# Attention of a hybrid encoder: heads begun under the input projections, windowed heads turned by a product with a diagonal

## The reference, cut to what matters

```
h = rms_norm(x) * (1 + scale) + shift
qa,ka,va,qd,kd,vd = split(h @ w_in)            # rotary on q and k
windowed (8 heads, 2 kv heads, width 64):  p = exp(s - m) / (sum + exp(sink - m));  o = p @ v
differential (4 heads of 2 maps, width 128): a = softmax(s1) - lam * softmax(s2);  o = rms_norm(a @ v)
x = x + gate * (concat(windowed, differential) @ w_out)
```

## Time and profile before

| | us |
|---|---|
| median of three runs | 1367.25 (1365.81 to 1367.95) |
| profiled execution | 1363.22 |
| its span | 1361.5 |
| TensorE busy | 1288.9 (95%) |
| VectorE, ScalarE busy | 452.0, 292.9 |
| mean granted TensorE clock | 0.984 |

### The profile page before, as it was taken

The page is one execution under the profiler, slowest core; times in us unless marked ns, Lnnn a source line. Parts: engine busy times, 40 slices in busy tenths (PEclk is TensorE's granted clock), DMA queues, the critical chain, the costliest instruction groups (busy, mean ns, idle before and its releaser), DMA issues.

```text
span 1361.5 us, 21859 instructions
## 1 busy us (share of the span) xinstructions
PE 1288.9 (95%) x9514; PEld 714.5 (52%) x9515; DVE 452.0 (33%) x808; ACT 292.9 (22%) x524; POOL 32.8 (2%) x82
## 2 busy tenths in 40 slices
PE   5999999999999989996689999999999999899997
PEld 5766888787888677441233333444354333244342
DVE  4876867777459665200100120001001110000011
ACT  3346544443433462110010000010010000010010
POOL 1102100000001010000000000000000000000000
PEclk9999999999999999998789999999999999899999
DMA  9988748888436757999999999999999999999996
GB/s 349 326 338 329 233 176 311 311 297 309 174 123 208 307 204 306 378 408 424 418 421 423 422 421 419 403 408 421 423 419 421 421 424 421 419 420 421 422 423 259
DMA packets 93044, 481.95 MB, mean 354 GB/s; under 512 B 8808, under 2 KB 10928, under 8 KB 63248
## 3 DMA queue, kind: packets, MB, share of 16 engines
q1 hardware_dynamic: 88992, 475.06, 86.9%
q10 hardware_dynamic: 2720, 2.93, 0.8%
q0 software_dynamic: 1232, 2.50, 0.8%
HBM read 477.32 MB, written 1.05 MB: 351 GB/s over the span
## 4 chain that ended last, share of the span: by engine, by line
PE 82%; DMA 9%; DVE 4%; SPq 2%; ACT 2%; issue 1%; POOL 0%; DVEq 0%; ACTq 0%
PE ps L2621 31%; PE ps L2671 15%; PE ps L2304 8%; PE ps L2306 8%; PE ps L2305 8%; DMA raws<-in_moe_w_down_dram 5%; DMA raw<-in_moe_w_gate_dram 2%; DMA weights<-in_ada_w_dram 2%; SPq L891 2%; PE ps L2687 2%; PE ps L2638 1%; DVE weights_lo L1376 1%; PE ps L2594 1%; PE ps L2385 1%; PE ps L2226 1%; PE ps L2370 1%
## 5 line engine op out<-in xcount | busy, mean ns | idle before, releaser
L2621 PE MATMUL ps<-raw,hX 128*32 128x384 f32 (+3 forms) x3840 | 473.0, 543 | 11.8 <-DMA raw<-in_moe_w_up_dram 8.4
L2621 PEld LDWEIGHTS ps<-raw,hX 128*32 128x32 f32 (+1 forms) x3840 | 162.0, 117 | 296.6 <-issue 267.3
L2671 PE MATMUL ps<-raws,m_actT 128*32 128x512 f32 (+1 forms) x1072 | 168.5, 604 | 9.9 <-DMA raws<-in_moe_w_down_dram 9.9
L2304 PE MATMUL ps<-weights_hi,hT_hi 128*128 128x512 f32 (+1 forms) x416 | 162.1, 390 | 2.6 <-DVE hT_lo L1482 1.4
L1797 DVE TENSOR_TENSOR m_act<-m_act,ps 128x512 f32<-128x512 f32 (+1 forms) x28 | 17.4, 621 | 432.0 <-PE ps L2621 431.2
L2306 PE MATMUL ps<-weights_hi,hT_lo 128*128 128x512 f32 (+1 forms) x416 | 159.0, 382 | 0.0
L2305 PE MATMUL ps<-weights_lo,hT_hi 128*128 128x512 f32 (+1 forms) x416 | 158.6, 381 | 0.0
L1376 DVE TENSOR_TENSOR weights_lo<-weights,weights_hi 128x2048 fp32r<-128x2048 f32 (+1 forms) x52 | 113.1, 2202 | 2.3 <-ACT weights_hi L1052 1.1
L2671 PEld LDWEIGHTS ps<-raws,m_actT 128*32 128x32 f32 (+1 forms) x1072 | 52.2, 123 | 116.3 <-issue 103.5
L1052 ACT ACTIVATE weights_hi<-weights 128x2048 fp32r<-128x2048 f32 (+1 forms) x48 | 87.2, 1840 | 55.9 <-PE ps L2306 51.3
L2304 PEld LDWEIGHTS ps<-weights_hi,hT_hi 128*128 128x128 f32 x416 | 78.2, 188 | 21.0 <-issue 4.8
(11 more groups left out here) (282 smaller groups left out, 1084.3 us busy)
## 6 DMA issues: line engine op xcount, KB each, us to landing
raw<-in_moe_w_gate_dram SPq DMA_DIRECT2D x64, 1024.0 KB, 16.5
raw<-in_moe_w_up_dram SPq DMA_DIRECT2D x64, 1024.0 KB, 22.1
raws<-in_moe_w_down_dram SPq DMA_DIRECT2D x32, 2048.0 KB, 24.7
raw<-in_moe_w_gate_dram SPq DMA_DIRECT2D x64, 768.0 KB, 23.3
raw<-in_moe_w_up_dram SPq DMA_DIRECT2D x64, 768.0 KB, 21.1
raws<-in_moe_w_down_dram SPq DMA_DIRECT2D x28, 1536.0 KB, 19.5
weights<-in_ada_w_dram SPq DMA_DIRECT2D x19, 2048.0 KB, 10.0
weights<-in_ffn_w_gate_dram SPq DMA_DIRECT2D x14, 1024.0 KB, 5.1
```

The lines of the kernel that those rows point to most:

```text
L2304: pe.matmul(dst, stat_hi, hi, start=start, stop=False, skip_group_check=True)
L2621: mm = pe.matmul(ps[tile * q:tile * q + tile, bank, 0:COL[n]], hX[:, i, at_row:at_row + tile], raw[buffer][:, at:at + COL[n]], start=(i == ...
L2671: mm = pe.matmul(ps[tile * q:tile * q + tile, bank, col:col + w], stationary[:, at_row:at_row + tile], rows_in[:, D * j + w * g:D * j + w ...
```

## The change

- **Head of the attention under the projections** (`HEAD_EARLY`, both layers): the turns of q and k, in a new order (`TURN_PAIRS`), the scores of steps 0 and 1 and the first modulation chunk are woven into the input products (3,1), (4,0) and (4,1). ScalarE makes all copies of q and k.
- **Windowed heads**: VectorE multiplies the identity by the reciprocals (`diag`), and TensorE's turn is a product of the probabilities with it, so they come out turned and scaled. `values` holds v stationary (64 columns) and streams the probabilities of both token halves, two heads side by side in the two column halves; the outputs come out turned and are split straight into `hTh` and `hTl` (`window_high`, `head_out`). Two of four turns of outputs fall away, and so do the `keep` products.
- **Output product (0,0)** runs in pieces between steps 6 and 7 (`first_out`). The weights of the second output chunk are split inside the attention in layer 1 (`OUT_SECOND_EARLY`), behind the last turn in layer 0.
- Modulation chunks move to later steps. The mask is added only where it can bite. Squares of the norm move to VectorE, and GpSimd's gate DMAs stand between its two powers.

```diff
-ADA_STEP = [[0, 1, 2, 3, 4, 5, 6, 7], [0, 1, 2, 3]]
+HEAD_EARLY = (True, True)
+ADA_STEP = [[1, 2, 3, 4, 5, 6, 7, 8], [1, 3, 5, 6] if HEAD_EARLY[1] else [0, 1, 2, 3]]
+OUT_SECOND_EARLY = (False, True)
...
+TURN_PAIRS = [(3, 5, 4, 0, 2, 6, 1) if early else tuple(range(QK_TILES // 2)) for early in HEAD_EARLY]
+ROPES_OF_PAIR = (4, 4, 4, 4, 6, 6, 8)
+PAIRS_OF_STEP = ((3, 5), (4, 6), (0, 2), (1, 2))
+BEFORE_HEAD = [IN_ORDER.index((3, 1)) if early else len(IN_ORDER) for early in HEAD_EARLY]
...
-                spread_gate(layer, 0)
                 for t in range(NT):
+                    if t:
+                        spread_gate(layer, 0)
...
+            def attention_head(layer):
+
+                for i in range(4):
+                    copy_qk(layer, i)
+                if layer == 0:
+                    lambda_exp()
+                straight_part("out", layer, 0, 0)
+                exponentials(layer, 0)
+                copy_qk(layer, 4)
+                copy_qk(layer, 5)
+                straight_part("out", layer, 0, 1)
+                copy_qk(layer, 6)
+                exponentials(layer, 1)
...
+                for j in range(2 if early else 0, PAIRS + 3):
+                    k = j - 2
                     if j == PAIRS:
-                        turned_high(3 * layer + 1, 0)
                         turned_high(3 * layer + 1, 1)
+                    if 0 <= k < PAIRS:
+                        copy_probs(k, 0)
+                    if k >= 1 and windowed(k - 1):
+                        window_high(k - 1)
+                    if 0 <= k < PAIRS and windowed(k):
+                        copy_probs(k, 1)
                     if j < PAIRS:
-                        u, q, par = PAIRS * layer + j, j % 4, j % 2
-                        act.wait_ge(max_done, u + 1)
-                        for n in range(4):
-                            e = act.activation(E[:, par, n, :], score_rows(par)[:, n, :], ACT.Exp,
-                                               bias=negm[:, q, n:n + 1], scale=SCALE, accum_out=sums[:, q, n:n + 1])
-                        if pair(2 * j) < 4:
-                            e = act.activation(sinke[:, q, :], sinkm[:, q, :], ACT.Exp)
-                        e.then_inc(exp_done, 1)
+                        exponentials(layer, j)
+                    if j == PAIRS and OUT_SECOND_EARLY[layer]:
+                        straight_part("out", layer, 1, 0)
+                turned_high(3 * layer + 1, 3)
+                if not OUT_SECOND_EARLY[layer]:
+                    straight_part("out", layer, 1, 0)
+                straight_part("out", layer, 1, 1)
...
-                    then(dve.tensor_tensor(rows, rows, mask[:, t, :].unsqueeze(1).broadcast_to([P, 4, SEQ]), ALU.add))
+                    far = slice(P - t * P, 2 * P - t * P)
+                    then(dve.tensor_tensor(rows[:, :, far], rows[:, :, far],
+                                           mask[:, t, far].unsqueeze(1).broadcast_to([P, 4, P]), ALU.add))
...
-                    dve.reciprocal(rec[:, q, :], den[:, q, :]).then_inc(probs_done, 1)
+                    then(dve.reciprocal(rec[:, q, :], den[:, q, :]))
+                    dve.tensor_tensor(diag[:, par], ident[:].unsqueeze(1).broadcast_to([P, 4, P]),
+                                      rec[:, q, :].unsqueeze(2).broadcast_to([P, 4, P]),
+                                      ALU.mult).then_inc(probs_done, 1)
...
+                        square, diff = xn[:, t, 0:WIN_WIDTH], xn[:, t, WIN_WIDTH:]
+                        then(dve.tensor_tensor(square, diff, diff, ALU.mult))
+                        then(dve.reduce_sum(ssq_d[:, four], square.rearrange("p (h n) -> p h n", h=N_DIFF), AX_X))
...
+                    if j == PAIRS + 1 and OUT_SECOND_EARLY[layer]:
+                        low_of("out", layer, 1, 0)
+                    if j == PAIRS + 2:
+                        turned_low(3 * layer + 1, 3)
+                        if not OUT_SECOND_EARLY[layer]:
+                            low_of("out", layer, 1, 0)
...
+                early = HEAD_EARLY[layer]
+                if early:
+                    maxima(layer, 0)
+                    low_of("out", layer, 0, 0)
                 rope(layer, 3, 1)
-                low_of("out", layer, 0, 0)
+                if early:
+                    probabilities(layer, 0)
+                else:
+                    low_of("out", layer, 0, 0)
                 rope(layer, 4, 0)
+                if early:
+                    maxima(layer, 1)
                 rope(layer, 4, 1)
+                if early:
+                    low_of("out", layer, 0, 1)
...
+                        if windowed(j):
+                            row = 2 * (n // 2) + half
+                            mm = pe.matmul(ps[:, 3, n * P:n * P + P], E[:, j % 2, row, keys], diag[:, j % 2, row, :],
+                                           start=True, stop=True)
+                        else:
+                            mm = pe.transpose(ps[:, 3, n * P:n * P + P], E[:, j % 2, n // 2, keys], ident[:])
...
+                    if windowed(j):
+                        col = (m // 2) * HEAD
                         for kt in range(NT):
-                            mm = pe.matmul(ps[:, j % 2, to:to + width], PT[:, i % 2, 2 * h + kt, :],
-                                           v[:, kt, col:col + width], start=(kt == 0), stop=(kt == NT - 1))
+                            for h in range(2):
+                                mm = pe.matmul(ps[HEAD * h:HEAD * h + HEAD, j % 2, 0:2 * P], v[:, kt, col:col + HEAD],
+                                               turned[:, :, 2 * h + kt, :], start=(kt == 0), stop=(kt == NT - 1),
+                                               skip_group_check=True)
...
+                if early:
+                    turn_qk(0)
+                    project("in", layer, 3, 1, range(0, 2))
+                    turn_qk(1)
+                    project("in", layer, 3, 1, range(2, 4))
+                    turn_qk(2)
+                    turn_qk(3)
+                    scores_of(0)
+                    project("in", layer, 3, 1, range(4, KD))
+                    project("in", layer, 4, 0, range(0, 4))
+                    turn_qk(4)
+                    project("in", layer, 4, 0, range(4, KD))
+                    turn_qk(5)
+                    project("in", layer, 4, 1, range(0, 4))
+                    scores_of(1)
+                    turn_qk(6)
+                    project("in", layer, 4, 1, range(4, KD))
+                    pe.wait_ge(qkT_done, 7 * layer + 7)
+                    ada_chunk(*ADA_LATER[layer][0])
+                    pe.wait_ge(rope_done, 2 * IN_CHUNKS * (layer + 1))
...
+                for j in range(2 if early else 0, PAIRS + 3):
                     if j < PAIRS:
                         scores_of(j)
+                    k = j - 2
+                    if 0 <= k < PAIRS:
+                        turn_probs(k, 0)
+                    if j == PAIRS:
+                        first_out(range(0, 2))
+                    if k >= 1:
+                        values(k - 1)
                     if j == PAIRS + 1:
-                        pe.wait_ge(mod_ready, 3 * layer + 3)
-                        keep(5, 2)
-                    a = 2 * (j - 2)
-                    if 0 <= a < UNITS:
-                        turn_probs(a)
-                    if a >= 2:
-                        values(a - 1)
-                    if 0 <= a < UNITS:
-                        turn_probs(a + 1)
-                        values(a)
+                        first_out(range(4, 6))
+                    if 0 <= k < PAIRS and windowed(k):
+                        turn_probs(k, 1)
+                    if j == PAIRS:
+                        first_out(range(2, 4))
+                    if j == PAIRS + 1:
+                        first_out(range(6, KD))
                     for c, (of, n) in enumerate(ADA_LATER[layer]):
                         if ADA_STEP[layer][c] == j:
                             ada_chunk(of, n)
                     if j == PAIRS - 1:
                         pe.wait_ge(mix_done, N_DIFF * (NT * layer + 1))
                         pe.wait_ge(exp_done, PAIRS * layer + PAIRS - 1)
-                        turn_rows_of(3 * layer + 1, 0)
                         turn_rows_of(3 * layer + 1, 1)
+                pe.wait_ge(mix_done, N_DIFF * (NT * layer + 2))
+                turn_rows_of(3 * layer + 1, 3)
```

226 lines of the change are left out of this document (126 added, 100 removed).

## The result

The changed kernel takes 1370.47 us (median of 10 runs, 1365.41 to 1372.01) against 1366.13 us for the kernel before on the same chip (1363.82 to 1369.88): ratio 1.003, 95% interval 1.0019 to 1.0041. The forecast was 3.2 us faster, 1364.0; it is some 4 us slower, outside the range.

The account below looks back on a forecast made before the run. The expert phase was taken as bound by its weight stream, its start tied to TensorE in the mixers. Layer 1's 4.9 plus layer 0's 0.3 less 2.0 for the clock gave 3.2 us, so 1364.0; own range 1362 to 1366.

Parts of the forecast that it names:

- 0.7 us of waiting in the walk, up to 3: Layer 0's attention: six later modulation chunks land about when used, so TensorE waits 0.7 us, up to 3.
- The walk: Step-by-step run through three engine queues in both mixers, each instruction starting when ready; trusted to a microsecond for known operations.
- layer 0's chunks land late: Rival: layer 0's last three modulation chunks each land 1 us later than forecast, giving 1367 us; chance 0.1.
- waits on DMA for modulation weights in layer 0: Sign named in advance that would show the forecast wrong, in layer 0's attention; no size given.
- the sum: Layer 0, (3,1) to (1,0): TensorE work 62.9 us plus waits 1.2 and 5.0, starting at 71.45 and ending at 140.6.
- the late split: Before layer 0's output product (1,0): TensorE idles 5.0 us because its weights are split only behind the last turn.
- the clock behind it: Behind layer 0's 5 us wait the granted clock falls, costing 2.0 us, between none and 2.4.
- the windowed turns and values: Windowed steps, both layers: eight turns as diagonal products take 1.9 us a step, values with v stationary 1.06.
- layer 1's waits: Layer 1's mixer: TensorE waits 2.1 us at step 3, 1.6 at step 8 and 2.2 for (1,0)'s second half.
- The column halves overlap: Rival claimed they do not: windowed values take 1.85 us instead of 1.06, giving 1370.1 us, slower; chance 0.1.
- The rival by which the stream does not start earlier: Expert weight stream's head, not TensorE, sets the rate, so the end moves by 0.3 us: 1367; chance 0.1.
- Layer 1: Layer 1's mixer, (3,1) to (1,0): forecast 4.9 us gained, (1,0) at 505.2 to 505.5 against 510.4.

Follow-up runs that it names:

- chunks_quarter: Changed kernel loading only a quarter of each of layer 0's modulation chunks 6 to 11, same TensorE work; total 1717.93 us says nothing, as tokens go to other experts.
- loads_in_gap: Changed kernel with ScalarE's transfers of router weights, final scale and biases issued earlier, in layer 0's head; 1367.73 us, 1.0009 of the kernel before.
- fillers: Changed kernel with 36 ident by ident products in layer 0's 4.90 us wait and 16 in layer 1's 2.07 us wait; 1370.90 us.
- head0_off: Changed kernel with layer 0's head as in the kernel before, layer 1 keeping the whole change; 1365.72 us, 0.9992 of the kernel before.
- chunks_in_head: Changed kernel with modulation chunks 4 and 5 used inside layer 0's head and their slots refilled at once; 1367.98 us, 1.0013 of the kernel before.
- split0_early: Changed kernel with layer 0's second output chunk split before the last turned rows, as in layer 1; 1364.04 us, 0.9988 of the kernel before.
- heads_off_split: Changed kernel with both layers' heads as before, layer 0's split early and 9 fillers in its wait; 1362.62 us, 0.9975 of the kernel before.
- four_repairs: Changed kernel with chunks 4 and 5 in layer 0's head, chunk steps reordered, layer 0's early split with 9 fillers, and layer 1's VectorE swap; 1357.85 us.
- the swap: Changed kernel with VectorE doing step 1's probabilities ahead of step 2's maxima in layer 1; alone 1366.62 us, 1.0005 of the kernel before.
- four_without_fill: Same as four_repairs but without the 9 fillers in the middle of layer 0's (1,0); 1357.83 us, 0.9944 of the kernel before.

## Why the prediction was wrong

**The step that failed** is the one that put layer 0's chunks at "0.7 us of waiting in the walk, up to 3". They waited 6.17 us, and chunks_quarter puts their price at 6.5. The walk had the cause, spare slots that come free with the last input product, and the pace: from the first (101.14) to the last (131.54) the six chunks land 6.1 us apart. It had three other terms wrong. The slots were to come free 17.4 us after the start of (3,1) (88.8 less 71.45); it was 18.3 (91.14 less 72.86). The first chunk was to follow at the pace of the others, 6.1 us; it took 10.0, with a second chunk, the router weights, the final scale and the biases in flight beside it (without these three 7.7, and (1,0) 2.2 us earlier, in loads_in_gap). And the steps were to take about 6 us; the two ahead of the waits at 120.55 and 126.61 take 4.6 and 4.5 without them. The rival "layer 0's chunks land late" was the right mechanism, sized at 3 us and given 0.1, and "waits on DMA for modulation weights in layer 0" stood among the signs of being wrong.

**Layer 0's head** has a second error, 0.99 us before the sixth turn of q and k. Its chain can be read on ScalarE (first two rows) and VectorE:

```profile
78.36 1.28 ACT L1145 ACT_TABLE_LOAD   x1
79.65 0.21 ACT L1145 ACTIVATE lame<-lams 128x4 f32<-128x4 f32 x1
```

```profile
79.89 0.16 DVE L1482 TENSOR_TENSOR neglam<-lame 128x2 f32<-128x2 f32 x1 [2.39 <-ACT lame L1145]
...
85.48 0.42 DVE L1636 COPY v<-ps 128x256 f32<-128x256 f32 x1
```

The exponential of lambda now stands behind ScalarE's four copies, and a table load comes right ahead of it. Before, that load lay in ScalarE's idle time:

```profile
67.34 1.28 ACT L1310 ACT_TABLE_LOAD   x1
```

VectorE waits 2.39 us for the exponential, where it waited 0.27 before, and then goes without a recorded wait through the maxima, the split and the rotation up to the copy of v that TensorE waits for. No run moves the exponential alone, so this cause is read from the trace and not tested. With the other small waits and breaks this makes (3,1) to (1,0) 76.04 us (72.86 to 148.90) where the sum had 69.1; TensorE's work in it, without the 12.27 us of waits, is 63.8 against the forecast 62.9. So 6.9 us are missing here, 5.5 of them in the waits for chunks and 1.0 in this one.

**Right in size**: the late split, 5.0 forecast and 4.90 measured; the clock behind it, 2.0 and 1.9 (fillers); the windowed turns and values; layer 1's waits, 2.1, 1.6 and 2.2 against 2.07, 1.55 and 2.14. The column halves overlap, so that rival is out. The rule in the Trainium skill, TensorE: Matmul & The Clock Gate, Terms, by which a turn as a product would take four times a transpose, would have cost 3.9 us a step. The trace shows 0.99 to 1.09 for four turns, so 2.0 to 2.2 for the eight of a step, twice the 0.49 of four transposes in the earlier trace rows: the page's factor does not hold for this shape. The rival by which the stream does not start earlier is out as well: the next expert loads are issued at 519.29, with layer 1's (1,0), and the first expert product moves with layer 1.

**Layer 1** was forecast at 4.9 and gave 3.77 (453.69 to 546.12 against 443.68 to 539.88). What was missed is the clock: I charged it only to the 5 us wait, and it falls behind the 2.07 us wait as well, in five of the six traces that have this wait (changed, head0_off, chunks_quarter, loads_in_gap, chunks_in_head; not split0_early), for 1.5 us. The walk was right about the wait and had nothing on what follows it.

**Where the gain is.** With both heads as before, the rest of the change (windowed steps, output products between the last steps, half masks, copies and squares on other engines) brings 1.0 us in layer 0, with its split early and fillers, and 2.9 in layer 1 (heads_off_split). Which single edit brings the 2.9 was not taken apart. Layer 1's head adds 0.8 us as it stands, and 3.9 together with the swap. Layer 0's head costs 4.6 as it stands (309.67 against 305.03): its late chunks cost 6.5, and what it gives with the chunks in time is 1.9 us by chunks_quarter and 0.4 by four_repairs, from one trace of each kernel.

## What to carry to other kernels

A step that is used as filler early gives back its slots late: before work is interleaved ahead of the last use of a buffer, write down which loads hang on that buffer, and look whether the queue stands empty meanwhile and what other transfers will then start beside them. Here every wait of TensorE of 2 us or more could bring a half clock of 1.5 to 1.9 us behind it, so such a wait is to be priced twice, with and without. And a large rearrangement is better timed in parts, and each part again once the wait that it brings is gone: layer 1's head looked worth 0.8 us, and with one swap on VectorE the two are worth 3.9. One flag for the split (2.95 us in layer 0's trace) gave more than layer 0's head in any form.

## What the hardware showed

- The granted clock falls behind waits of 2.07 to 2.16 us as behind 4.90, but not always. Behind the 2.07 us wait in layer 1 it was 0.71 in one trace and 1.00 in another, and it fell in five of six; behind the 2.14 to 2.16 us inside layer 1's (1,0) it fell in one of fourteen; behind the 4.90 us wait without fillers in all seven (0.50 to 0.61 in the lowest 5 us). Length alone does not decide: it fell behind 2.52 us in loads_in_gap and held behind 3.01 us in fillers. It does not fall in the wait alone: in four_without_fill the first three products behind it are at 0.23 us, and 0.43 comes from 144.39 on. The Trainium skill (TensorE: Matmul & The Clock Gate, Part 1) has the clock throttled after idleness. The falls in the two mixers agree, each comes in or behind a wait of 2.07 us or more; the one some 40 us into the expert phase has no wait of TensorE before it.
- With the same code and the same weights to load, the expert phase of 822 us differs by up to 3.2 us between traces, which is the size of the effects looked for; whether that one fall comes is worth 1.7 us of it (9.65 against 7.96). Cuts at marks inside the trace were needed to see the rest.
